# 32 unused bytes ahead of the split activations in SBUF

## The reference

```
p = einsum('bsd,dk->bsk', h, w_in[l])
a = einsum('becd,edf->becf', xe, w_gate_e);  u = einsum('becd,edf->becf', xe, w_up_e)
y = einsum('becf,efd->becd', silu(a) * u, w_down_e)
x = x + (silu(h @ w_gate[l]) * (h @ w_up[l])) @ w_down[l]
```

## Time and profile before

| | |
|---|---|
| median of three timed runs | 2134.13 us (2130.15 to 2134.3) |
| the profiled execution | 2127.52 us, its span 2125.6 us |
| mean granted clock | 0.892 |
| PE busy | 1698.7 us, 80% |
| PE weight loads | 1230.6 us, 58% |
| DVE, ACT, POOL busy | 808.9, 646.7, 84.0 us |
| DMA | 613.49 MB, mean 289 GB/s |

### The profile page before, as it was taken

One profiled execution on the slowest core, in us unless ns is written; L12 is line 12 of the kernel. 1 busy time (PEld: TensorE's weight loads), 2 busy tenths in 40 slices (PEclk: granted clock), 3 DMA queues, 4 the chain that ended last, 5 costly groups with the idle time before them and its releaser, 6 DMA issues.

```text
span 2125.6 us, 32653 instructions
## 1 busy us (share of the span) xinstructions
PE 1698.7 (80%) x13430; PEld 1230.6 (58%) x13430; DVE 808.9 (38%) x1592; ACT 646.7 (30%) x1144; POOL 84.0 (4%) x143
## 2 busy tenths in 40 slices
PE   5999975656665665666665799988999999999998
PEld 3889921211111221111111599988989988989996
DVE  2374621001101111100111457775656654666654
ACT  3334310000000000000000347654754434655433
POOL 2000010000000000000000200101100001000000
PEclk9999988877878778777778799999999999999999
DMA  9986789999999999999999853408065545146650
GB/s 367 334 317 230 287 366 428 429 429 427 429 429 429 429 429 429 427 429 428 429 429 429 321 199 120 140 18 285 21 197 165 195 170 179 53 139 189 198 179 20
DMA packets 152994, 613.49 MB, mean 289 GB/s; under 512 B 8816, under 2 KB 62138, under 8 KB 128312
## 3 DMA queue, kind: packets, MB, share of 16 engines
q1 hardware_dynamic: 148928, 604.47, 72.4%
q0 software_dynamic: 3200, 7.14, 1.2%
q10 hardware_dynamic: 760, 0.39, 0.1%
HBM read 610.88 MB, written 5.03 MB: 290 GB/s over the span
## 4 chain that ended last, share of the span: by engine, by line
PE 54%; DMA 38%; DVE 3%; ACT 1%; issue 1%; SPq 1%; DVEq 1%; POOL 0%; POOLq 0%; ACTq 0%
PE psum L1473 52%; DMA ring<-in_w_down_e 19%; DMA ring<-in_w_up_e 18%; DMA ring<-in_w_in 1%; PE psum L1843 1%; DVE ring_r L704 1%; SPq L750 0%; ACT arena L1070 0%; ACT ring_r L695 0%; PE psum L1578 0%; SPq L769 0%; DVE arena L2448 0%; POOL stat L945 0%; PE psum L2007 0%; PE psum L1992 0%
## 5 line engine op out<-in xcount | busy, mean ns | idle before, releaser
L1473 PE MATMUL psum<-ring,arena 128*32 128x512 f32 (+2 forms) x4314 | 537.6, 643 | 279.9 <-DMA ring<-in_w_up_e 128.1
L1473 PE MATMUL psum<-xR_r,ring_r 128*128 128x256 f32 x4416 | 542.9, 281 | 2.1 <-DVE xR_r L2087 1.3
L1473 PEld LDWEIGHTS psum<-xR_r,ring_r 128*128 128x128 f32 x4416 | 521.0, 188 | 12.7 <-issue 10.8
L1473 PEld LDWEIGHTS psum<-ring,arena 128*32 128x32 f32 x4314 | 155.3, 134 | 629.8 <-issue 211.9
L704 DVE TENSOR_TENSOR ring_r<-ring,ring_r 128x1024 fp32r<-128x1024 f32 (+2 forms) x332 | 377.9, 1172 | 192.0 <-ACT ring_r L695 191.3
L695 ACT CAST ring_r<-ring 128x1024 fp32r<-128x1024 f32 (+2 forms) x332 | 320.3, 1007 | 382.1 <-PE psum L1473 377.9
L1473 PE MATMUL psum<-arena 128*128 128x256 f32 (+7 forms) x1270 | 188.0, 374 | 21.2 <-DVE arena L2323 9.9
L2320 DVE TENSOR_TENSOR arena<-arena,psum 128x512 f32<-128x512 f32 x16 | 16.9, 1055 | 476.8 <-PE psum L1473 476.8
L1473 PE MATMUL psum<-ring_r,xR_r 128*128 128x256 f32 (+3 forms) x1344 | 170.8, 284 | 10.5 <-DVE xR_r L2072 6.9
L1473 PE MATMUL psum<-ring_r,arena_r 128*128 128x512 f32 (+1 forms) x912 | 168.2, 346 | 2.1 <-DVE mt L2699 2.1
L1473 PEld LDWEIGHTS psum<-ring_r,xR_r 128*128 128x128 f32 x1344 | 160.6, 191 | 13.2 <-DVE ring_r L704 7.2
(11 more groups left out here) (270 smaller groups left out, 959.6 us busy)
## 6 DMA issues: line engine op xcount, KB each, us to landing
ring<-in_w_gate_e SPq DMA_DIRECT2D x64, 2048.0 KB, 25.9
ring<-in_w_down_e SPq DMA_DIRECT2D x63, 2048.0 KB, 26.4
ring<-in_w_up_e SPq DMA_DIRECT2D x62, 2048.0 KB, 24.9
ring<-in_w_in SPq DMA_DIRECT2D x30, 2048.0 KB, 12.5
ring<-in_w_ada SPq DMA_DIRECT2D x12, 2048.0 KB, 13.8
ring<-in_w_gate SPq DMA_DIRECT2D x22, 1024.0 KB, 5.5
ring<-in_w_up SPq DMA_DIRECT2D x22, 1024.0 KB, 8.2
ring<-in_w_down SPq DMA_DIRECT2D x10, 2048.0 KB, 7.8
```

The source lines that it names most:

```text
L1473: return nc.tensor.matmul(o, l, r, start=s, stop=e)
```

## The change

One line declares a tensor of 8 float32 values in each partition between `stat` and `xR`. No instruction reads or writes it. Everything that is declared after it (`xR`, `mt2`, the arena) begins 32 bytes further on; what is declared before it stays.

```diff
@@ -303,6 +303,7 @@
         vec1 = sb("vec1", 112)
         vec2 = sb("vec2", 78)
         stat = sb("stat", 512)
+        sb("apart", 8)
         x_moe, xR = twice("xR", 2 * KT * T)
         xR = xR.rearrange("p (c k t) -> p c k t", c=2, k=KT)
         mt2 = sb("mt2", 2 * 512)
```

## The result

The changed kernel takes 2152.88 us (median of four executions, 2152.43 to 2155.32), the kernel before 2134.04 us (2130.15 to 2134.3): ratio 1.0097, 95% interval 1.0081 to 1.0113. It is slower by 18.8 us, where 2127 us was forecast and the range ended at 2148. The profiled execution took 2152.43 us with a span of 2150.6 at a granted clock of 0.898; the one of before took 2127.52 us with 2125.6 at 0.892. The two spans differ by 25.0 us, more than the medians: the profiled execution of before was quicker than its four timed ones.

The account below looks back on a forecast made before the run. Bound: expert weight transfers from about 300 to 1183 us, PE's matmul pace around them. Terms -7.3 + 0 + 0 gave 2120.2 us from the profiled 2127.5; from the median, 2134.1 - 7.3 = 2126.8, forecast 2127 us, range 2116 to 2148.

Parts of the forecast that it names:

- the terms of 0: VectorE and ScalarE work on shifted rows: 0, ends -1 and +2 us; expert weight transfers: 0, 1.5 us either way.
- Moving operand, and the two paces: Split-product matmuls moving xR or the arena: 1,456 of 2,240 spaced 118.6 ns would run at 113.6 ns, -7.3 us.
- The stationary operand: PE matmuls whose held operand lies in a shifted tensor: cost 0, ends -5.0 and +5.0 ns a matmul.
- longer read: Shifted moving rows, read in 64-byte pieces, span 17 instead of 16: 20.4 us slower, 2155 us; chance 0.10.
- Tight runs turning loose: Both gate/up runs of 1008 matmuls slow by 5.0 ns each: 10.1 us, with others 15.6; 2144 to 2150 us; chance 0.15.
- No change: A matmul run's start fixes its pace and 32 bytes matter to nothing: 2132 us; chance 0.33.

## Why the prediction was wrong

**What was right.** No instruction, wait or transfer changed. VectorE's and ScalarE's splitting kept its speed (1222 and 1046 ns where before has 1222 and 1047), and so did the expert stage (429 GB/s), as the terms of 0 said. The reading that matmul pace is what the time after 1183 us hangs on held, as did the observation that the same addresses run in two paces: the kernel with all tensors 32 further on showed gate/up loose at unchanged distances, and the one with the arena alone moved showed it at unchanged addresses.

**The step that failed** is the one called "Moving operand, and the two paces": "If the 32 bytes between the streams take away what holds a run in the loose pace, the gain has its ceiling at 2,640 x 5.0 = 13.2 us", with 65% of 2,240 loose matmuls tightened, -7.3 us. The lever was named rightly, the bytes between the streams, and its sign was a guess. Its reason, that the loose runs have both streams at multiples of 64, holds for the tight gate/up runs as well, on the same two tensors, and so couldn't tell the paces apart. (Sorting all runs of 12 or more by the spacing of their second halves gives 2,478 loose matmuls in the moved forms and not 2,240; the term would have been 8.1 us.) The tight pace is what the distance of before allows, while 12 of 16 distances in the gate/up form never showed it. At 32 no stream and no run of that form was tight: gate/up rose to 120.1 ns, the loose runs by 0 to 2.2 ns. The term, forecast at -7.3 us, measured +18.9 us over its forms (4416 and 480), against a profiled execution of before that had both gate/up runs tight.

**The stationary operand**, taken as 0 with ends of 5 ns, cost 6.4 ns in the 512-column form and 3.5 ns in ring_r,xR_r, 7.4 us with 528 and 1,152 matmuls. Its evidence, the kw run at 3.06 us against 3.07, compared one loose run with another, and a loose run hardly shows a shift (0 to 2.2 ns above).

**The rival "longer read"** came nearest in time (2155 us, with gate/up near 121.7), by a mechanism that is wrong: the 512-column runs did not keep 60.1 us, a shift of both streams by 32 or 64 costs nothing, and 64 bytes off the old distance cost nearly what 32 cost. **"Tight runs turning loose"** was nearer in kind: the tight pace was lost, but to a third, slower pattern of 120 ns and not to 118, and the rival had no reason why. The flip to 118 does exist without any shift: gate/up was loose, at 118.99 us, in the kernels with all tensors and with the arena alone moved. **"No change"** leaned on the Trainium skill's "Advanced Engine Details and Errata", section "SBUF Cachelines", by which 32 bytes leave each operand's place in its 16-byte lines as it was. The measurement decides: they cost up to 6.7 ns a matmul here. The Trainium skill's page "SBUF — State Buffer", section "SBUF: two separate sides", says that PE never waits on anyone at its ports. For other engines this case agrees: a loose gate/up run beside a busy VectorE has 117.8 ns, and so has the isolated stream with VectorE idle. Whether PE's two streams are each other's obstacle no run shows.

**Left open:** what in PE or SBUF has the period of 256 bytes, why a run at shift 0 or 128 starts tight or loose (six different leads at 0 always gave loose in the isolated streams, yet the profiled execution of before was tight in both layers), and why 320 columns take 146.6 ns at every shift.

## What to carry to other kernels

When matmuls of 256 or 512 float32r columns follow each other without a gap, the number of bytes between the stationary and the moving tensor is a tuning parameter of up to 6% of their pace at 256 columns and 3% at 512, with a period of 256 bytes in the streams measured here; alignment by itself is none. Sweep it with isolated streams of the real forms in steps of 16 bytes, one column for each form and for each of the two roles, and then place the tensors. And any change that adds or drops a small tensor shifts this distance: a loss or gain of up to one per cent after such an edit may be nothing but that.

## What the runs showed of the hardware

- The spacing of 128x256 float32r matmuls at a granted clock of 1.00 lies between 113.3 and 120.1 ns for shifts in steps of 16 bytes (123.2 in one stream), and goes by the distance of the two operands modulo 256 bytes and by the form; shifts by 4 and 8 bytes gave 121.6 and 120.9 ns.
- At some distances two paces exist, 113.3 and 117.8 ns (116.7 and 117.8 at shift 224), and a stream keeps its own over 480 and 1008 matmuls.
- The best pace is 0.443 ns a column at 256 and at 512 moving columns, and in the simple form the worst of the five shifts lose 6.8 ns a matmul at both (120.1 and 233.5 ns).
- 48 matmuls with 32 stationary columns take no less time than with 128 at 256 moving columns (5.70 to 5.90 us).
- With 320 moving columns the spacing was 146.5 to 146.7 ns at all five shifts.
